# Function tables of ScalarE loaded ahead of the waits, one set for logarithm and exponential, and four norm stages by feature tile

## The reference

```python
def _rms_heads(o, norm_g):                       # end of the hgrn branch
    return o * lax.rsqrt(mean(o * o) + RMS_EPS) * norm_g
...
kk = _heads(k * k_k)                             # rwkv branch, keys
kk = kk * lax.rsqrt(jnp.sum(kk * kk, axis=-1, keepdims=True) + 1e-12)
...
yn = (y - mu) * lax.rsqrt(var + GN_EPS) * gn_g + gn_b   # rwkv readout
out = yn + bonus
...
log_alpha = -exp(a_log) * softplus(a + dt_bias)  # gated deltanet
o = rms_norm(o, norm_g) * silu(gate)
...
def conv_ffn(h, w_up, conv_w, w_down):
    g, u = jnp.split(dwconv(h @ w_up, conv_w), 2, axis=-1)
    return (jax.nn.silu(g) * u) @ w_down
```

## Time and profile before

| | |
|---|---|
| Median of three executions | 3210.45 us |
| The three | 3210.97, 3210.45, 3204.51 us |
| Span of the profiled execution, first to last instruction | 3209.5 us |
| PE busy | 2595.8 us, 81% |
| DVE busy | 1538.1 us, 48% |
| ACT busy | 1020.6 us, 32% |
| POOL busy | 733.8 us, 23% |
| Table loads on ACT | 98, 1283 ns each |

### The profile page before, as it was taken

How to read it: one execution, slowest core, us unless ns; L and a number is a source line. 1 busy time by engine, 2 the same in 40 slices (tenths; PEclk the granted TensorE clock), 3 DMA queues, 4 the chain that set the end, 5 groups by cost and what they waited for, 6 DMA issues and landing times. The chain is left out here.

```text
span 3209.5 us, 60192 instructions
## 1 busy us (share of the span) xinstructions
PE 2595.8 (81%) x25070; PEld 2118.1 (66%) x25070; DVE 1538.1 (48%) x2455; ACT 1020.6 (32%) x1590; POOL 733.8 (23%) x443
## 2 busy tenths in 40 slices
PE   2843498477686679977877889999998899889998
PEld 1733477277475557866766768888886744567886
DVE  6677759433533776424444244314415344544242
ACT  2332232421322353252223244312224322254232
POOL 4001100031041222212030422222242200434444
PEclk9976699588598889998998899999998999889999
DMA  5420055000000544310001111211112300422222
GB/s 202 148 76 2 2 198 190 9 3 3 1 3 2 184 169 140 105 42 2 3 2 80 53 66 59 74 51 65 64 54 86 109 1 1 144 91 98 86 96 87
DMA packets 62131, 228.74 MB, mean 71 GB/s; under 512 B 5984, under 2 KB 12384, under 8 KB 60128
## 3 DMA queue, kind: packets, MB, share of 16 engines
q1 hardware_dynamic: 61920, 225.66, 20.4%
HBM read 212.00 MB, written 13.63 MB: 70 GB/s over the span
## 5 line engine op out<-in xcount | busy, mean ns | idle before, releaser
L2499 POOL TENSOR_TENSOR f_wl<-f_stage,f_wh 128x1024 fp32r<-128x1024 f32 (+1 forms) x120 | 316.4, 2636 | 611.7 <-ACT f_wh L2495 611.7
L2495 ACT ACTIVATE f_wh<-f_stage 128x1024 fp32r<-128x1024 f32 (+1 forms) x120 | 137.6, 1147 | 595.8 <-PE f_ps L2599 593.1
L2599 PE MATMUL f_ps<-h_h,f_wh 128*128 128x256 f32 (+1 forms) x704 | 238.3, 341 | 14.5 <-POOL f_wl L2499 13.2
L2764 DVE SCALAR_TENSOR_TENSOR f_xr<-f_ps,cols,f_xr 128x511 f32<-128x511 f32 (+1 forms) x132 | 83.1, 657 | 339.5 <-ACT f_xr L2757 338.9
L2599 PE MATMUL f_ps<-h_l,f_wh 128*128 128x256 f32 (+1 forms) x704 | 237.6, 340 | 0.0
L2599 PE MATMUL f_ps<-h_h,f_wl 128*128 128x256 f32 (+1 forms) x704 | 237.6, 339 | 0.0
L2599 PE MATMUL f_ps<-f_f_ah,f_wl 128*128 128x512 f32 (+1 forms) x528 | 183.7, 355 | 0.0
L2599 PE MATMUL f_ps<-f_f_ah,f_wh 128*128 128x512 f32 (+1 forms) x528 | 183.6, 355 | 0.0
L2599 PE MATMUL f_ps<-f_f_al,f_wh 128*128 128x512 f32 (+1 forms) x528 | 183.5, 354 | 0.0
L2599 PEld LDWEIGHTS f_ps<-h_h,f_wh 128*128 128x128 f32 x704 | 133.2, 190 | 32.4 <-POOL f_wl L2499 14.4
L2599 PE MATMUL f_ps<-hc_h,f_wh 128*128 128x512 f32 x352 | 142.1, 404 | 14.4 <-POOL f_wl L2499 14.2
(11 more groups left out here) (651 smaller groups left out, 6694.9 us busy)
## 6 DMA issues: line engine op xcount, KB each, us to landing
f_stage<-in_ffn_up SPq DMA_DIRECT2D x88, 512.0 KB, 3.3
f_stage<-in_ffn_down SPq DMA_DIRECT2D x32, 704.0 KB, 4.0
a_in_stage<-in_ab_w SPq DMA_DIRECT2D x25, 512.0 KB, 3.6
p_hgrn_side_w<-in_ada_w SPq DMA_DIRECT2D x12, 1024.0 KB, 4.9
u_in_side_w<-in_ada_w SPq DMA_DIRECT2D x11, 1024.0 KB, 5.1
u_in_stage<-in_w_in SPq DMA_DIRECT2D x21, 512.0 KB, 3.5
mod_w<-in_mod_w SPq DMA_DIRECT2D x8, 1024.0 KB, 13.8
a_in_side_w<-in_ada_w SPq DMA_DIRECT2D x8, 1024.0 KB, 7.6
```

Of the source, the lines that this page charges most:

```text
L2495: self.nc.scalar.activation(self.wh[:, slot, :w], self.stage[:, slot, :w], ACT.Copy).then_inc(self.w_high, 1)
L2499: self.nc.gpsimd.tensor_tensor(self.wl[:, slot, :w], self.stage[:, slot, :w], self.wh[:, slot, :w].bitcast(F32), ALU.subtract).then_inc(se ...
L2599: done = self.nc.tensor.matmul(out[s][:, :tn], w, x[:, k, t0:t0 + tn], start=k == 0 and n == 0, stop=k == job.kt - 1 and n == 2)
L2764: nc.vector.scalar_tensor_tensor(out, b[:, :n - 1], self.tap(part, 0, i), out, ALU.mult, ALU.add).then_inc(self.before_ok[part], 1)
```

## The change

ACT's program names its table sets itself, by 24 instructions that load a set (10 more are placed by the compiler): `LN_EXP` (one set that holds Ln and Exp), `SIGMOID` and `SILU`. They stand ahead of waits or of other work of ACT, and the compiler adds a load only where the set in use does not hold the next function. ACT's program had 61 load instructions and has 34 now, and none stands in a loop.

Second, head_rms, rwkv_common, rwkv_readout and unit_norm go feature tile by feature tile: each Square, product, Ln, Exp and multiplication is issued for one tile and signals for one tile. In rwkv_common the Tanh goes last, behind a load of its set. In rwkv_readout the products v go ahead of b, and the affine step goes from DVE to ACT (`Identity` with a scale and a bias per partition).

Third, functions that nothing calls and blank lines are removed, so the line numbers of the change are lower. The instructions of SP and POOL, and but for what is told here those of PE and DVE, stay as they are.

```diff
 def head_rms ...
-            nc.scalar.activation(sq[:, :, :], o[:, :, :], ACT.Square).then_inc(squared, 1)
-            act.wait_ge(mean, NR)
             for f in range(NR):
+                nc.scalar.activation(sq[:, f, :], o[:, f, :], ACT.Square).then_inc(squared, 1)
+            for f in range(NR):
+                act.wait_ge(summed, f + 1)
                 nc.scalar.activation(sq[:, f, :], ps[f][:, :], ACT.Ln, scale=1.0 / HD, bias=eps_col(t, 1e-6)
                                      ).then_inc(log_ok, 1)
-            act.wait_ge(log_ok, NR)
-            nc.scalar.activation(sq[:, :, :], sq[:, :, :], ACT.Exp, scale=-0.5).then_inc(root, 1)
+                act.wait_ge(log_ok, f + 1)
+                nc.scalar.activation(sq[:, f, :], sq[:, f, :], ACT.Exp, scale=-0.5).then_inc(root, 1)
...
 rwkv_common, ACT
-            nc.scalar.activation(th[:, :], u[:, 9, :], ACT.Tanh)
...
+            nc.scalar.preload_act_table_set(SIGMOID)
+            nc.scalar.activation(th[:, :], u[:, 9, :], ACT.Tanh)
...
 rwkv_front, ACT
             gates(0)
             gates(1)
+            nc.scalar.preload_act_table_set(LN_EXP)
             decays(0)
             decays(1)
+            nc.scalar.preload_act_table_set(SIGMOID)
             tokens(0)
             gates(2)
+            nc.scalar.preload_act_table_set(LN_EXP)
             outputs(0)
             decays(2)
+            if d == 0:
+                nc.scalar.preload_act_table_set(SIGMOID)
             tokens(1)
...
 rwkv_readout, ACT
+            for f in range(NR):
+                act.wait_ge(scaled, f + 1)
+                nc.scalar.activation(y[:, f, :], y[:, f, :], ACT.Identity, scale=col(t, "rwkv_gn_g", f),
+                                     bias=col(t, "rwkv_gn_b", f)).then_inc(affine, 1)
...
 the FFN stage, ACT
-            for part in range(2):
-                ffn.credits(act, part)
-                row.on_act(act, ffn.up[part])
-                row.on_act(act, ffn.down[part])
+            nc.scalar.preload_act_table_set(SILU)
+            ffn.credits(act, 0)
+            row.on_act(act, ffn.up[0])
+            row.on_act(act, ffn.down[0])
+            ffn.credits(act, 1)
+            row.on_act(act, ffn.up[1])
+            nc.scalar.preload_act_table_set(LN_EXP)
+            row.on_act(act, ffn.down[1])
             rms.inverse_root(act)
```

More of the change, by code:

```diff
@@ L67, in __exit__ @@
         return False
[L70 to L82, removed]
 def open_clock(nc, lhs, rhs, bank, n):
@@ L89, in open_clock @@
         nc.tensor.matmul(bank[:, :rhs.shape[-1]], lhs, rhs, start=True, stop=True)
[L92 to L199, removed]
-                    dve.wait_ge(tile_done, i + 3)
-                else:
-                    dve.wait_ge(act_done, i + 1)
-                ins = evac_dve(dve, i, ps[slot * ns:slot * ns + ns], slot)
-                if ins is not None:
-                    ins.then_inc(banks_free, 1)
-            tile_loop(dve, n_tiles, step)
-        @block.tensor
-        def _(pe):
-            pe.sem_inc(tile_done, 2)
-            t0, n = spans[-1]
-            def products(i, slot, last):
-                pe.wait_ge(w_low, i + 3)
-                pe.wait_ge(banks_free, i + 1)
-                for s, (t0, n) in enumerate(spans):
-                    out = ps[slot * ns + s][:, :n]
-                    for k in range(kt):
-                        w_hi = wh[:, slot, k * P:(k + 1) * P]
-                        w_lo = wl[:, slot, k * P:(k + 1) * P]
-                        nc.tensor.matmul(out, w_hi, xh[:, k, t0:t0 + n], start=k == 0, stop=False)
-                        nc.tensor.matmul(out, w_hi, xl[:, k, t0:t0 + n], start=False, stop=False)
-                        done = nc.tensor.matmul(out, w_lo, xh[:, k, t0:t0 + n], start=False, stop=k == kt - 1)
-                done.then_inc(tile_done, 1)
-            tile_loop(pe, n_tiles, products)
@@ L796, in _ @@
         def _(act):
+            if table:
+                nc.scalar.preload_act_table_set(table)
             for j in range(0, len(jobs), 2):
@@ L1157, in hgrn @@
     to_tokens(nc, "hgrn_vt", [([p[:, 3 + f, i * P:(i + 1) * P] for f in range(NR)], vt[:, i, :])
-                              for i in range(TT)], ident)
+                              for i in range(TT)], ident, LN_EXP)
     w = {
@@ L1763, in rwkv_readout @@
         root = st.sem("root")
+        scaled = st.sem("scaled")
+        affine = st.sem("affine")
         own = st.sem("own")
@@ L1781, in _ @@
                 nc.tensor.matmul(mps[f % 2][:, :], heads, y[:, f, :], start=True, stop=True).then_inc(mean_ok, 1)
+            for f in range(NR):
+                pe.wait_ge(squared, f + 1)
+                nc.tensor.matmul(vps[f][:, :], heads, sq[:, f, :], start=True, stop=True).then_inc(var_ok, 1)
             pe.wait_ge(rb_ok, 1)
@@ L1934, with unit_norm @@
 ALPHA = float(2.0 ** 0.25)
-def unit_norm(nc, t, name, x, nf, spans, mat, mult, eps, factor, before=None, also=()):
+def unit_norm(nc, t, name, x, nf, spans, mat, mult, eps, factor, also=()):
     jobs = [(f, t0, n) for f in range(nf) for t0, n in spans]
```

305 lines of the change are left out of this document (48 added, 257 removed).

## The result

The change takes 3174.14 us in the median of four executions (3165.71 to 3177.92), against 3210.71 us before (3204.51 to 3217.32): ratio 0.9882, interval 0.986 to 0.9905. That is 36.6 us faster, where 34.7 were forecast. A sum that comes out so near can still have wrong terms, and this one has.

What follows compares the result with a forecast made beforehand. PE, busy 81% of the span, bounds the kernel; ACT's loads count only where PE or a barrier waits. 13.0 + 5.0 + 5.2 + 7.7 + 5.3 - 1.5 = 34.7 us off 3209.5, plus 0.95 for the median: 3176 us, range 3160 to 3192.

Steps and rivals of the forecast that it cites:

- three signs: Prediction wrong if FFN stages become shorter, a stage by tile keeps its length, or granted clock moves by over 0.005.
- A load costs 1.28 us where nothing lies beside it: Norm ends: ten exposed loads at 1.28 us, plus 0.1 us in each of the last two norms; 13.0 us gained.
- w_out: two loads, 2.57: End of w_out: two exposed loads, 1.28 us each, come off the path.
- The FFN loops: 0: Forty loads in the FFN loops, twice 25.7 us, cost nothing because PE's windows there are full; gain 0.
- hgrn_rms 5.2, rwkv_common 7.7, rwkv_readout 5.3: Gains in us from working these three stages feature tile by feature tile.
- the possible gain from the clock: hgrn_rms: PE's products bound the stage and could be shorter at a higher clock; by tile, up to 3 us.
- gdn_rows with the next stage's head, and c_in: 3.1 and 1.9: Loads ahead of DVE's steps go: 3.1 us (1.3 to 3.9) and 1.9 us (0 to 2.57), together 5.0.
- a_in: 0: Loads in a_in lie beside PE's products, so removing them gains 0; 1.28 us each without that cover.
- o_rms: 0: The stage ends with the transfer of x_b, which the change does not touch, so no gain.
- rwkv_front: a loss of 1.5: Added SIGMOID load ahead of tokens(1), d = 0, loses 1.28 us; tokens(0) loses 0 to 0.4 per direction.
- The third rival: PE granted the lower clock longer behind shortened stages: 1.3% loses 35 us, 2% gives 3227 us; chance 3%.
- the first rival: All removed loads count, the FFN loops' 51 us partly too: gain 50 to 86, 3124 to 3160 us; chance 4%.

Runs made afterwards that it cites:

- e1: The change with the four norm stages put back as before, table loads kept as in the change: 3180.09 us, ratio 0.9909 to before.
- e2: The kernel before with the four norm stages by feature tile and no table load named by the program: 3217.72 us, ratio 1.0025 to before.
- e3: The kernel before with one line added, loading SILU ahead of the loops of both FFN stages: 3210.86 us, ratio 1.0007.
- e6: The change with one more 1536 KB transfer, read by nothing, ahead of x_b in o_rms: 3172.31 us in one run.
- e9: The change with rwkv_common alone put back (one Square, six Ln, one Exp), its Tanh still last: 3171.24 us, ratio 0.9878.
- e5: The change with unit_norm (stage o_rms) put back to all Ln, then all Exp: 3168.52 us in one run.
- e8: The change without the load of SIGMOID ahead of tokens(1) in rwkv_front, d = 0: 3166.25 us, ratio 0.9861.
- e7: The change with the affine step of rwkv_readout back on DVE, tile by tile: 3175.93 us in one run.

## Why the prediction was right

The forecast of 3176 us and the range held, but two of the three signs by which the prediction said it would be wrong came up: the FFN stages became shorter by more than their ends (1.9 us in the last one's loop), and the mean granted clock moved by more than 0.005. By its steps:

- **A load costs 1.28 us where nothing lies beside it.** Right. hgrn_prep gave 2.57 and 1.27 us, hgrn_rms and rwkv_readout 1.28 and 1.29 in e1; the first FFN, from barrier to barrier, 1.17 to 1.30. The last FFN's end gave 1.37 (29.46 us before and 28.09 in the change from the last copy of weights on), with 1.38 forecast. c_out gave 1.30, 1.33 and 1.07 us in the three profiles of the change, with 1.38 forecast, though it is up to 0.7 us longer than before in e2 and e3, which leave it alone. In p_hgrn and ab_out the load is not told apart: ab_out is 1.65 us shorter in e2 too, where it is before's.
- **w_out: two loads, 2.57.** Not told apart from the spread (0.52, 0.35 and 3.85 us). In the change's profile the wait for PE ahead of its first Ln grew from 1.74, behind a load of 1.28, to 4.60 us.
- **The FFN loops: 0.** Right for the first FFN (e3: +0.02), wrong for the last, where they cost 1.87 us in its first loop (the rest of e3's 3.27 us goes with PE's clock). The step that failed is the reading of PE's busy time and of its chain of waits as proof that nothing delays it. The wait stood in the weight loads.
- **hgrn_rms 5.2, rwkv_common 7.7, rwkv_readout 5.3.** 4.19, 8.07 and 5.5 to 5.7. The first was mis-sized in PE's three products, 5.49 us and not 4.54. In e6 they took 2.84 us, and the stage was 1.9 us shorter again: the possible gain from the clock that the prediction named.
- **gdn_rows with the next stage's head, and c_in: 3.1 and 1.9.** 0.8 (1.68 less 0.88), which is under the lower bound of 1.3, and 1.0 to 1.3. In gdn_rows alone 1.68 us came off, not far above DVE's idle time of 1.32: that the rest of the two loads had been filled by copies of DVE's own fits this and was not tried. In gdn_common the load at the head gave nothing when it went, and the stage is 0.87 to 0.92 us longer in all programs with the new tables. The first product there is a 0.45 us row in the change and 0.31 before; but it is 0.45 in e3 too, where the stage is only 0.32 us longer, so the clock at the head makes part of it and the rest is open.
- **a_in: 0.** It gave 0.9 to 1.2 us in every profile with the new tables (e1 and e9 too), 0.07 in e2 and 0.35 in e3. Which of its loads was exposed was not tried.
- **o_rms: 0.** Right, and shown by e5 and e6.
- **rwkv_front: a loss of 1.5.** The stage of d = 0 is 1.4 us longer, but of that the early load is only 0.8 (e8). The rest goes with PE's clock, which here moves 3.4 us. For d = 1 the stage is 1.4 to 3.5 us shorter, not longer.
- **Not forecast: gdn_inv of d = 0**, 2.1 to 2.9 us shorter in every profile with the new tables. Its first quarter, by windows, before:

```profile
1475.20:1491.20 16.00, 12.18 (x196) 9.25 (x196) 3.22 (x6) 1.98 (x6) 7.17 (x10) 0.71 0.01 2
```

and in the change:

```profile
1454.90:1470.20 15.30, 10.62 (x223) 7.99 (x225) 3.22 (x6) 2.63 (x8) 8.79 (x13) 0.90 0.01 2
```

The granted clock is 0.90 there in the place of 0.71. All eleven profiles with the new tables have the gain (2.1 to 2.9 us) and e2 and e3 do not, so it goes with the tables. The rows show that it comes with the clock; why, they do not show.

The errors of the terms, as gain over the forecast: +3.0 in the last FFN (1.9 of it the loads), +2.5 in gdn_inv, +1.1 in a_in, about +2.8 in rwkv_front, +0.4 in rwkv_common and +0.3 in rwkv_readout, against -2.3 in gdn_rows, -1.0 in hgrn_rms and -0.7 in c_in. That leaves some 6 us, and the three medians of the change (3170 to 3174) lie 2 to 6 us under the forecast. The number was near partly by luck: what was forecast too high was made up by gains that nobody had forecast, some of which came with PE's clock (gdn_inv, the third weight tile of the last FFN). The third rival was right in kind: stages behind the changed ones were granted another clock, by up to 3 us a stage, but in both directions (worse in rwkv_front of d = 0, better in gdn_inv), not the 35 us on one side that it needed. Of the first rival, that the loads in the FFN loops count, 1.9 us of its 51 were true. The mean granted clock rose from 0.901 to between 0.907 and 0.912 in the executions of the change.

## What to carry to other kernels

Name the table sets by hand where Ln and Exp take turns, and only then split the norm into tiles: the split without the joint set was slower than no split (e2). PE's busy time is no proof that it isn't held up; look at the idle time of its weight loads as well, and compare the pace of the same loop with and without the suspect. When a stage gets shorter, find where in it the gain stands before giving it to the edit: 1.4 of the 3.3 us of e3 stood where a program without the edit had gained as much. Where a stage is followed by others whose length moved with the clock, as rwkv_front did, do not count its gain as the program's, and repeat the profile before explaining a difference of 3 us.

## What the runs showed of the hardware

- A table load took 1283 ns in every row, and where nothing else was waited for the next activation's row began 1.29 to 1.30 us after the load's.
- The same instructions gave stages that fall on discrete lengths: rwkv_front of d = 0 took 77.2 us (the change) or 73.8 (e6, alike up to there), with a granted clock of 0.50 or 0.72 in its second quarter. hgrn_rms took 9.04 or 7.15 us, with three products of 5.49 or 2.84 us. The third weight tile of the last FFN took 8.64 us before and in e9 and 6.8 to 7.1 in all the others.
- Activations with a scale and a bias per partition took 2.22 us for three rows of 512 on ACT; the same step on DVE took 1.45 us.
- In one profile (e7) the attention stage was 8.5 us longer than before with nothing changed in it. The cause is not known.
